# Retention queries and keys turned by SBUF-to-SBUF strip transfers in place of rotation products, with regrouped dense work, earlier input loads and in-place reads

## What is computed

```python
# first block, cut
h = rmsnorm(x); proj = h @ w_in
y_a = chunked_relpos_attention(a_q, a_k, a_v, rel_bias)   # 8 heads of 64
y_b = hgrn2_recurrence(b_q, b_f, b_i, b_g, ...)           # gated recurrence, 8 heads
y_c = mla_attention(c_q, c_kv, c_kr, positions, ...)      # latent attention, 8 heads
x = x + sum(sigmoid(gates) * (y @ w_branch)) @ w_out
x = x + square(relu(rmsnorm(x) @ w_ff1)) @ w_ff2
# second block, two layers, cut
fox  = forgetting_attention(fq, fk, fv, f_logit)
rq_h = apply_rotary(rq); rk_h = apply_rotary(rk) * HEAD_DIM ** -0.5
ret  = silu(rg) * head_group_norm(retention(rq_h, rk_h, rv))
h = h + concat(fox, ret) @ w_out
h = h + gated_conv_ffn(rms_norm(h)) ; h = h + sigmoid(rms_norm(h) @ w_gate) * (p @ w_proj)

def apply_rotary(t, cos, sin):      # halves of 32 of each head of 64
    t1, t2 = split(t)
    return concat([t1 * c - t2 * s, t1 * s + t2 * c])
```

## Time and profile before

| | us |
|---|---|
| median of three runs | 2422.09 |
| lowest, highest | 2421.88, 2429.56 |
| the profiled execution | 2421.89 |
| its span, first to last instruction | 2420.1 |
| granted TensorE clock over the span | 0.995 |
| first matmul | 14.11 |
| first attention | 87 to 217 |
| recurrence | 222 to 359 |
| latent attention | 404 to 527 |
| forgetting attention, layer 1 and 2 | 1061 to 1198, 1767 to 1904 |

### The profile page before, as it was taken

The page is one execution under the profiler, slowest core; times in us unless marked ns, Lnnn a source line. Parts: engine busy times, 40 slices in busy tenths (PEclk is TensorE's granted clock), DMA queues, the critical chain, the costliest instruction groups (busy, mean ns, idle before and its releaser), DMA issues.

```text
span 2420.1 us, 35839 instructions
## 1 busy us (share of the span) xinstructions
PE 2362.6 (98%) x11542; PEld 1861.7 (77%) x11542; DVE 1109.2 (46%) x1851; ACT 883.2 (36%) x1377; POOL 1193.1 (49%) x1572
## 2 busy tenths in 40 slices
PE   7998999999999999999999999999999999999997
PEld 5776776667888888877778888887877678888885
DVE  4366765433323214536664334344346655242444
ACT  3355444444322223424433222245334243222254
POOL 5344554235564455543326555466533245555564
PEclk9999999999999999999999999999999999999998
DMA  4221112114332232321313323323322223323232
GB/s 152 91 86 45 44 53 66 53 53 130 96 113 89 94 104 87 99 96 61 98 43 104 104 88 103 94 81 104 105 70 62 88 70 97 112 87 104 85 93 92
DMA packets 62829, 211.49 MB, mean 87 GB/s; under 512 B 7008, under 2 KB 7392, under 8 KB 62736
## 3 DMA queue, kind: packets, MB, share of 16 engines
q1 hardware_dynamic: 56160, 194.27, 25.6%
q10 hardware_dynamic: 6576, 15.97, 2.0%
HBM read 208.06 MB, written 2.16 MB: 87 GB/s over the span
## 4 chain that ended last, share of the span: by engine, by line
PE 37%; issue 32%; POOL 26%; DVE 2%; POOLq 2%; ACT 1%; DMA 1%; DVEq 0%; ACTq 0%; SPq 0%
POOL w_lo L1840 25%; PE acc L270 11%; PE acc L272 10%; PE acc L271 10%; POOLq L1869 1%; PE sc L416 1%; PE po L364 1%; PE pt L346 1%; PE sc L644 0%; DMA raw<-in_w_in 0%; PE acc L625 0%; POOL qcur L1866 0%; DVE act_lo L1224 0%; PE sc L468 0%; DVEq L1314 0%
## 5 line engine op out<-in xcount | busy, mean ns | idle before, releaser
L1840 POOL TENSOR_TENSOR w_lo<-raw,w_hi 128x256 fp32r<-128x256 f32 x1506 | 1146.1, 793 | 1198.1 <-ACT w_hi L736 1196.2
L270 PE MATMUL acc<-act_hi,w_hi 128*128 128x512 f32 x1768 | 715.0, 404 | 20.3 <-DVE act_lo L1224 15.5
L272 PE MATMUL acc<-act_hi,w_lo 128*128 128x512 f32 x1768 | 691.1, 391 | 0.0
L271 PE MATMUL acc<-act_lo,w_hi 128*128 128x512 f32 x1768 | 690.2, 390 | 0.0
L736 ACT CAST w_hi<-raw 128x1024 fp32r<-128x1024 f32 (+1 forms) x390 | 392.3, 1016 | 380.1 <-PE acc L272 201.0
L270 PE MATMUL acc<-y_hi,w_hi 128*128 128x512 f32 x1108 | 446.3, 403 | 0.9 <-POOL w_lo L1840 0.9
L272 PE MATMUL acc<-y_hi,w_lo 128*128 128x512 f32 x1108 | 432.1, 390 | 0.0
L271 PE MATMUL acc<-y_lo,w_hi 128*128 128x512 f32 x1108 | 431.6, 390 | 0.0
L270 PEld LDWEIGHTS acc<-act_hi,w_hi 128*128 128x128 f32 x1768 | 332.5, 188 | 109.2 <-issue 33.5
L272 PEld LDWEIGHTS acc<-act_hi,w_lo 128*128 128x128 f32 x1768 | 332.6, 188 | 71.1
L271 PEld LDWEIGHTS acc<-act_lo,w_hi 128*128 128x128 f32 x1768 | 333.3, 189 | 65.5 <-issue 2.9
(11 more groups left out here) (313 smaller groups left out, 2113.3 us busy)
## 6 DMA issues: line engine op xcount, KB each, us to landing
raw<-in_w_ffn_wide SPq DMA_DIRECT2D x120, 512.0 KB, 3.5
raw<-in_w_in SPq DMA_DIRECT2D x104, 512.0 KB, 3.5
raw<-in_w_rest SPq DMA_DIRECT2D x72, 512.0 KB, 3.5
raw<-in_w_gate SPq DMA_DIRECT2D x24, 512.0 KB, 3.5
raw<-in_w_ple_gate SPq DMA_DIRECT2D x16, 512.0 KB, 3.5
raw<-in_w_branch SPq DMA_DIRECT2D x24, 256.0 KB, 2.7
raw<-in_w_ffn_narrow SPq DMA_DIRECT2D x16, 384.0 KB, 3.0
x<-in_x ACTq DMA_DIRECT2D x16, 256.0 KB, 3.6
```

Source lines behind the costliest of these rows:

```text
L270: nc.tensor.matmul(dst, w[0], src[0], start=start, stop=False)
L271: nc.tensor.matmul(dst, w[0], src[1], start=False, stop=False)
L272: return nc.tensor.matmul(dst, w[1], src[0], start=False, stop=stop)
L1840: last = nc.gpsimd.tensor_tensor(w_lo[:, slot, cut], raw[:, slot % 2, cut], w_hi[:, slot, cut], ALU.subtract)
```

## The change

- **Rotation.** `rope_r` and its products are gone. After evacuating q (or k) VectorE frees the bank; ScalarE's queue issues four DMAs of 32 partitions by 512 tokens from `wa` to `swapped` with the halves of each head exchanged; VectorE waits for all four, multiplies t by cos and the exchanged rows by sin (the sign of the first half is in the table now) and adds. q is turned at step 3 (was 2), k at step 4 (was 3), ahead of the gate's evacuation. The table `tab` stays the rotary one for the whole attention, so the first decay tile goes to `wb` and is loaded ahead of the attention.
- **Grouping.** A step of `softmax_pair` on TensorE is now: outputs of the tile before the last, scores, transposes of head 0, one share, transposes of head 1, one share.
- **In place.** The recurrence reads values and queries where they lie; no copies. Silu of the last pair moves after level 2 of pair 0.
- **Latent attention.** Sigmoids move to step 1 and totals to step 2 of the next pair.
- **Inputs.** SP issues the first two weight loads, four tiles of x and the constants ahead of its wait. The first `w_lo` is VectorE's, and the second cast comes after two tiles of the norm.

```diff
@@ -125,7 +125,7 @@
              [alias("s_ret2", "act_hi", [P, 1280]), alias("s_ret3", "act_hi", [P, 1280], skip=1280 * 4)]]
-    decay_tile = [tab] + [alias(f"decay{p}", "act_lo", [P, 2, T], skip=(p - 1) * 2 * T * 4) for p in range(1, PAIRS)]
+    decay_tile = [wb[:, 2:4, :]] + [alias(f"decay{p}", "act_lo", [P, 2, T], skip=(p - 1) * 2 * T * 4) for p in range(1, PAIRS)]
     v_ret = [vcur[:, :, :], kcur[:, 0, :].rearrange("p (t f) -> p t f", f=P)]
@@ -136,7 +136,7 @@
     vstage = qcur[:, 1, :]
-    rotated = wb[:, 1, :]
+    swapped = [wb[:, 0, :], wb[:, 1, :]]
     mean_bank = [po[:, :], pt[:, :], sc[:, 0, :], sc[:, 1, :]]
@@ -214,6 +214,14 @@
+    for j in range(2):
+        sp.dma_start(raw[:, j, :], dram["w_in1"][j]).then_inc(raw_loaded[j], 16)
+    for k in range(4, KD):
+        sp.dma_start(x[:, k, :], dram["x"][:, k, :]).then_inc(x_loaded[k], 16)
+    sp.dma_start(consts[:, :, :], dram["consts"]).then_inc(S("const_loaded"), 16)
+    sp.dma_start(masks[:, :, :], dram["masks"]).then_inc(S("const_loaded"), 16)
+    sp.dma_start(positions[:, :], dram["positions"].partition_broadcast(P)).then_inc(S("pos_loaded"), 16)
     sp.wait_ge(started, 1)
@@ -242,7 +250,7 @@
-    load(dram["w_in1"], 0, N_A, N_MA)
+    load(dram["w_in1"][2:N_MA], 0, N_A + 2, N_MA - 2)
     load_groups(4, N_MA, 0)
@@ -366,32 +374,31 @@
         at = 0
-        for qt in range(TT + 1):
-            share = iter(shares[qt])
-            def dense():
-                nonlocal at
-                n = next(share, 0)
-                for i in range(at, at + n):
-                    guest(i)
-                at += n
+        def dense(n):
+            nonlocal at
+            for i in range(at, at + n):
+                guest(i)
+            at += n
+        for qt in range(TT + 2):
+            if qt == 1 and values is not None:
+                pe.wait_ge(S("soft_ofree", 1), pair + 1)
+                transpose_values("soft", pair, po, src)
+            if qt > 1:
+                outputs(qt - 2)
             if qt < TT:
                 scores_of(qt)
-            dense()
-            if qt == 0 and values is not None:
-                pe.wait_ge(S("soft_ofree", 1), pair + 1)
-                transpose_values("soft", pair, po, src)
+            if 0 < qt <= TT:
+                transposes(2 * qt - 2)
+            if qt <= TT:
+                dense(shares[qt][0])
             if rope:
                 rope(qt)
-            if qt:
-                transposes(2 * qt - 2)
-                dense()
+            if 0 < qt <= TT:
                 transposes(2 * qt - 1)
-                dense()
-                outputs(qt - 1)
-                dense()
+                dense(shares[qt][1])
@@ -447,8 +454,8 @@
-    SHARES8 = ((6,), (1, 2, 2, 2), (1, 2, 2, 2), (1, 2, 2, 1), (2, 2, 2))
-    SHARES6 = ((6,), (1, 1, 2, 1), (1, 1, 1, 1), (1, 1, 1, 1), (1, 2, 2))
+    SHARES8 = ((6,), (3, 4), (3, 4), (3, 3), (3, 3))
+    SHARES6 = ((6,), (2, 3), (2, 2), (2, 2), (2, 3))
@@ -472,9 +479,7 @@
         softmax_pair(p, scores_a(p), guest_panels(p * 4 + N_B, N_B), SHARES8, p, src=wv[:, p, :])
-    pe.wait_ge(acc_free, N_MA + 4)
-    pe.wait_ge(S("soft_y"), PAIRS)
-    pe.wait_ge(S("b_qsilu"), PAIRS)
+    pe.wait_ge(acc_free, N_MA + 3)
@@ -485,6 +490,8 @@
                 pe.wait_ge(acc_free, n + 1)
+            if u == 2 and k == 0 and base == 0:
+                pe.wait_ge(S("soft_y"), PAIRS)
             if u == 2 and k == 0 and base == 4:
@@ -503,19 +510,19 @@
     LEVEL_SHARES = (2, 3, 3, 3, 3, 2, 2, 2, 2, 2)
-    with pe.Fori(0, PAIRS) as p:
+    for p in range(PAIRS):
         piece, at = merge_group(p * 4 + N_MA, 0), 0
-        pe.wait_ge(S("b_values"), p + 1)
-        transpose_values("b", p, pt, probs_t[:, 1, :])
+        transpose_values("b", p, pt, wv[:, p, :])
         for v, half in enumerate(LEVELS):
                 pe.wait_ge(S("b_k"), p + 1)
-                pe.wait_ge(S("b_q"), p + 1)
+                pe.wait_ge(S("b_qsilu"), p + 1)
             pe.wait_ge(S("b_sfree", 1), p * n_levels + max(v, 1))
             if v == 1:
+                pe.wait_ge(S("soft_ofree", 1), PAIRS + 1)
                 pe.wait_ge(S("b_ofree", 1), p + 1)
@@ -524,7 +531,7 @@
                     if half == 0:
-                        keys, queries = kcur[rows, 0, t * P:(t + 1) * P], tab[rows, 0, t * P:(t + 1) * P]
+                        keys, queries = kcur[rows, 0, t * P:(t + 1) * P], wa[rows, p, t * P:(t + 1) * P]
                     else:
@@ -618,22 +625,16 @@
-            def rope_r(qt):
-                if qt in (2, 3):
-                    j = qt - 2
-                    pe.wait_ge(S("r_qk"), pair * 2 + (j + 1))
-                    nc.tensor.matmul(acc[:, (O_R + j) % 4, :], c["rope"], wa[:, p + 4 * j, :],
-                                     start=True, stop=True).then_inc(S("r_rot"), 1)
                          SHARES8,
-                         pair + 4, src=wv[:, p, :], rope=rope_r)
+                         pair + 4, src=wv[:, p, :])
         pe.wait_ge(acc_free, layer + (N_BLOCK1 + O_O + 4))
             pair = l * 4 + p
+            pe.wait_ge(S("r_rotused"), pair * 2 + 2)
             if p:
@@ -722,11 +723,8 @@
     act.dma_start(params[:, :], dram["params"]).then_inc(S("param_loaded"), 16)
-    for k in range(KD):
+    for k in range(4):
         act.dma_start(x[:, k, :], dram["x"][:, k, :]).then_inc(x_loaded[k], 16)
-    act.dma_start(consts[:, :, :], dram["consts"]).then_inc(S("const_loaded"), 16)
-    act.dma_start(masks[:, :, :], dram["masks"]).then_inc(S("const_loaded"), 16)
-    act.dma_start(positions[:, :], dram["positions"].partition_broadcast(P)).then_inc(S("pos_loaded"), 16)
     act.wait_ge(started, 1)
@@ -834,10 +832,11 @@
     high(0, 0, 0)
-    high(0, 0, 1)
     act.wait_ge(S("param_loaded"), 16)
         norm_tile(0, k, k % 2, "mix_g")
+        if k == 1:
+            high(0, 0, 1)
     three_more(0, 0, N_A)
@@ -870,10 +874,8 @@
         in_place(ACT.Ln, "b_mixed", "b_mixedlog", p, tmp)
-    if qt == 4:
-        in_place(ACT.Silu, "b_g", "b_gsilu", p, wb[:, p + 4, :])
-        nc.scalar.activation(wa[:, p, :], wa[:, p, :], ACT.Silu).then_inc(S("b_qsilu"), 1)
-        ln_exp_table()
+    if qt == 4 and not last:
+        silus_b(p)
@@ -886,12 +888,6 @@
-    def values_b(p):
-        nc.scalar.copy(probs_t[:, 1, :], wv[:, p, :]).then_inc(S("b_values"), 1)
-    def queries_b(p):
-        nc.scalar.copy(tab[:, 0, :], wa[:, p, :]).then_inc(S("b_q"), 1)
@@ -913,22 +909,18 @@
             nc.scalar.activation(e1, src, ACT.Exp).then_inc(S("b_e"), 1)
+            if n == 2 and not p:
+                silus_b(PAIRS - 1)
             if n == 2 and p:
                 key_b(p + 1)
-            if n == 6 and not last:
-                values_b(p + 1)
-        if not last:
-            act.wait_ge(S("b_s", 1), p * n_levels + 10)
-            queries_b(p + 1)
-    act.wait_ge(S("soft_pv", 1), 4 * PAIRS + 1)
+    act.wait_ge(S("b_keyed"), PAIRS)
+    settle(act)
     key_b(0)
-    values_b(0)
-    queries_b(0)
     for p in range(PAIRS):
@@ -989,17 +981,21 @@
     act.drain().then_inc(S("c_v"), 1)
-    with act.Fori(0, PAIRS) as p:
+    def gates_mb(p):
+        for j in range(2):
+            in_place(ACT.Sigmoid, "m_z", "m_gate", p * 2 + (8 + j), tab[:, j, :])
+        ln_exp_table()
+    for p in range(PAIRS):
         def gates_and_weights(qt):
                 high(p * 2, p * 4, N_MB + LOOK + j, 512 if j < 2 else 1024)
-            if qt == 4:
-                for j in range(2):
-                    in_place(ACT.Sigmoid, "m_z", "m_gate", p * 2 + (8 + j), tab[:, j, :])
-                ln_exp_table()
+            if qt == 1 and p:
+                gates_mb(p - 1)
         softmax_pair(p + 4, gates_and_weights)
+    gates_mb(PAIRS - 1)
@@ -1055,6 +1051,7 @@
     act.dma_start(tab[:, :, :], dram["rotary"]).then_inc(S("rotary_loaded"), 16)
+    act.dma_start(decay_tile[0], dram["decay"][0]).then_inc(S("decay_loaded0"), 16)
     act.wait_ge(S("cum_stored"), l * 32 + 32)
@@ -1070,10 +1067,13 @@
                 aug_rows(p + 1)
-            if qt == 4 and last:
-                act.wait_ge(S("r_rotused"), l * 8 + 8)
-                settle(act)
-                act.dma_start(tab[:, :, :], dram["decay"][0]).then_inc(S("decay_loaded0"), 16)
+            if qt in (2, 3):
+                j = qt - 2
+                act.wait_ge(S("r_qk"), pair * 2 + (j + 1))
+                for to in range(0, P, HD // 2):
+                    at = to ^ (HD // 2)
+                    act.dma_start(swapped[j][to:to + HD // 2, :], wa[at:at + HD // 2, p + 4 * j, :]
+                                  ).then_inc(S(f"r_swap{j}"), 16)
             if qt == 4:
@@ -1309,6 +1309,8 @@
     norm_start()
+    dve.wait_ge(hi_done, 1)
+    v.tensor_tensor(w_lo[:, 0, :], raw[:, 0, :], w_hi[:, 0, :], ALU.subtract).then_inc(S("first_lo"), 1)
     for k in range(KD):
@@ -1384,6 +1386,7 @@
                 v.tensor_copy(key, less)
+                dve.drain().then_inc(S("b_keyed"), 1)
```

(37 more changed lines are left out.)

4 lines of the change are left out of this document (added).

## The result

| | before | after |
|---|---|---|
| median of the runs, us | 2422.09 | 2410.48 |
| lowest, highest | 2421.86, 2429.56 | 2406.44, 2412.73 |
| the profiled execution, its span | 2421.89, 2420.1 | 2412.61, 2410.7 |
| granted clock, mean of the span | 0.995 | 0.991 |

The ratio of after to before is 0.9945, 95% interval 0.9929 to 0.9961. The forecast was 2396.4 us, a gain of 25.5; the gain is 11.6 (9.3 between the two profiled executions), and the time lies 1.5 us above the upper end of the range. The direction was right, the size less than half.

A forecast was written before the change was run, and what follows sets the result against it. TensorE, with matmuls in flight for 98% of the span, was taken to bound the kernel. The terms −4.2 −6.3 +1.0 −2.7 +0.9 −13.8 −7.6 +7.2 summed to −25.5: 2396.4 us, range 2383 to 2409.

The forecast's parts named there:

- start: Input loads and first casts: ScalarE issues fewer loads, first matmul near 9.3 instead of 14.11; 4.2 us gained, between 2 and 6.
- first attention to level 1: Last attention outputs to the recurrence's level 1: values read in place, nothing but PE precedes the transposes; 6.3 us gained, bounds 3 and 7.
- Silu in pair 0: Recurrence pair 0: the last pair's gates, now after level 2, cost 1.0 us, between 0 and 2.
- latent borders: Latent attention's pair borders: waits for the exponential go, −2.7 us; VectorE late at tile 3's row maximum, +0.9.
- rotation products: Forgetting attention: sixteen products of 0.86 us go from TensorE, −13.8 us; called the surest term.
- grouping: All 16 attention pairs: 112 fewer borders of dense work at 0.07 us each, −7.6 us, between 0 and −24.
- border stop: Forgetting attention's pair borders: keys' turn delays VectorE's last evacuation; PE stalls 1.2 us at six borders, +7.2, between 0 and 12.
- (b): Rival: the exchange's four strips land in series, k two us past VectorE's need in all eight pairs; +16, 2412 us; chance 0.11.
- (a): Rival: no border stall in forgetting attention, and dense borders cost more than 0.07 us; 2385 us; chance 0.17.
- (c): Rival: slower than before, VectorE waiting at least 4.1 us for each of eight exchanges of k; up to 2457 us; chance 0.04.
- (d): Rival: start gains nothing (bytes bound it), level 1 waits for VectorE; +2.2 and +3.3, 2402 us; within the forecast's 0.68.
- The likeliest case: The forecast itself, whole kernel, together with (d): 2392 to 2404 us; chance 0.68.

The follow-up runs named there:

- early_old_latent: turn_early with gates and sums of the latent attention back behind the last step of each pair: 2395.22 us, ratio 0.9876.
- parts_products: low_parts with the rotation by products put back and no exchange: 2397.59 us, ratio 0.9882.
- early_old_groups: turn_early with TensorE's order and shares of before in every attention pair, 16 dense pieces instead of 9: 2403.02 us, ratio 0.9906.
- turn_early: The changed kernel with the exchange and the sums that follow it one query block earlier: 2394.73 us, ratio 0.9876.
- parts_gate_first: low_parts with VectorE evacuating the gates ahead of turning the keys at block 4: 2401.44 us, ratio 0.99.
- after_again: The changed kernel unedited, run again beside the others: 2408.57 us, ratio 0.9934.
- low_parts: The changed kernel with GpSimd's last weight panel of each recurrence pair in four quarters behind levels 6 to 9: 2398.07 us, ratio 0.9892.
- early_parts: The changed kernel with both the edits of turn_early and low_parts: 2383.45 us, ratio 0.9822.

## Why the prediction was right in direction and wrong in size

The terms of the sum, in us; "measured" is from the profiles of before and after, or from the run named.

| term | forecast | measured |
|---|---|---|
| start | −4.2 | −3.9 (first attention at 82.82, before 86.68) |
| first attention to level 1 | −6.3 | −6.5 |
| Silu in pair 0 | +1.0 | +2.0 |
| latent borders (−2.7 and +0.9) | −1.8 | −1.7 (early_old_latent) |
| rotation products | −13.8 | −13.6 (parts_products) |
| grouping | −7.6 | −8.3 (early_old_groups) |
| border stop | +7.2 | +11.9 |
| stretches at 1.2 GHz | none | +10.7 |

The second is counted up to level 1 of the recurrence: it comes 13.1 us sooner than before, the last attention pair 5.9, and 0.7 of the difference is grouping. The third is pair 0 from there to its end. The border stop is 6 × 1.98 (below). The stretches are 2.8 + 3.1 + 4 × 1.6 = 12.3, less the 1.6 of the one that the kernel before had behind its first forgetting attention. The measured column gives −9.4, with the 0.8 that the two latent edits bring only together −10.2; the last matmuls of the two traces differ by 9.7.

*What held.* Start, transition, products, grouping and latent borders came out within 1 us each in these profiles. The start is less certain than that: with nothing changed in it, the first attention begins between 82.1 and 84.0 us in the profiles here, and there is one profile of before. Silu in pair 0 took its upper bound: pair 0 got the stop of 0.8 us that was priced, and its stop at level 7 went from 0.4 to 1.35 as in the other pairs. Two readings were loose: the waits listed at the outset come to 48 us and not 40, and the wait of the last attention pair is 2.1, for the 2.4 is two waits. The signs came too: the first matmul at 8.73 (9.3 forecast), matmuls without gaps from 18.45 (near 20) and at 2.4 GHz from 21.27, level 1 after 4.3 us at a clock of 1.00, no row of L625. The first 9 us moved 267 GB/s where they had moved 228, and the strips landed 2.0 us after issue at the median, where the params load took 2.2. The Trainium skill's page "DMA: Bandwidth & Descriptors", section "Issuing engines are not separate DMA queues", lets the start gain issue time alone; the gain of 3.9 agrees, but no run here tells it from bytes moved sooner. The same page of the Trainium skill says in "Rules for kernel authors" that transfers to disjoint partition halves serialize. Here each strip landed 2.0 us after its own issue and the issues were 0.65 apart, so the fourth had landed 3.9 us after the first was issued; one whole transfer time after another, as (b) had it, would be 8.

*The step that failed first* is the price of the order on VectorE, 1.2 us per border. The forecast had the last evacuation 1.8 later, with 0.7 of slack. Measured against the moment at which TensorE was ready (1124.59 less its wait of 1.70), the evacuation stands 3.3 us ahead of it, before 5.7, so it came 2.4 later; less the slack of 0.7 that is the wait of 1.7. The keys' turn in front of it makes 1.9 of the 2.4, as forecast (3.2 us from the evacuation ahead of it, before 1.3). The rest is mostly a term that was left out: the turn in the block ahead now takes 3.0 us from 1113.34 to the next evacuation at 1116.35, where it had taken 2.65. The price of the exchange is in it, for the second product of a turn reads the exchanged rows from SBUF where it had read a bank of `acc`. It took 1.21 to 1.22 us in the eight cases in which it started while GpSimd was subtracting, as at 1114.09, and 0.68 in the eight in which GpSimd was idle; before, all sixteen took 0.68, with GpSimd subtracting beside each. And the wait is not all: pairs with a border stop take 34.5 us where those of turn_early take 32.55, so a stop costs 2.0, six times. The forecast also named the chain by evacuation, Silu and exponential as the one strictly in order; by parts_gate_first the row maxima on the same VectorE are as late, and Silu ahead of them takes nothing off the wait.

*The step that was missing* is what a stop does behind itself, a term put at nothing and measured at 10.7 us. I read 0.81 in the gap before the recurrence and priced it away there, but took every other stop at its length alone. The changed kernel has six new ones, five of 1.7 us and one of 1.2, and keeps two of the recurrence's per pair, listed at 0.8 and 1.35 (1.67 in pair 2, 0.74 in the last); behind some of them the clock fell to 1.2 GHz for 3.4 or 6.8 us, in 27.2 us of the profiled execution. The four profiles with border stops (after, after_again, low_parts, parts_gate_first) all have a stretch inside the forgetting attention, the nine others have none there. With the longer of the recurrence's stops gone, in six profiles, none has a stretch in the recurrence. In early_parts, which keeps the shorter one of 0.8, none is left anywhere between start and tail. The length of a stop does not settle it: in eight profiles, that of before among them, a stretch of 3.4 came within 7 us behind a forgetting attention, where the longest listed stop is 0.8. Why the recurrence's stops, which the kernel before had too, drew stretches of 6.8 us in four profiles (the changed kernel twice, turn_early, early_old_latent) and none in three (before, products, early_old_groups) is open; that is too few to call it the change's doing.

*The rivals and the signs.* The forecast's own sign of being wrong came: the forgetting attention is longer than before, by 0.2 us in layer 1 and 1.9 in layer 2. (a), no border stop: false as placed. (b), late strips, gives 2412, close to what was measured, and is false all the same: no wait on a strip. (c) fell with it. (d): the start gained its 3.9. The likeliest case was right in kind, with one term 4.7 short and one of 10.7 missing. On which side of the range's upper end a run falls is up to the stretches: the changed kernel's runs go from 2406.4, inside it, to 2412.7.

## What to carry over

On an engine that is full, price a new stop by its length and by the time behind it: here 1.7 us cost 2.0, and 1.6 to 3 more where the clock fell after it. Removing ten short stops gave 27 us beyond the change and a time that repeats within 0.6 us; here the spread of the runs was itself a sign of stops. Ask of each edit at which block its work stands: the exchange was worth nothing in one place and 14 us one block earlier. And when work moves to another engine's time, look at what runs beside it there.

## What the hardware showed that was not expected

The stretches come in two lengths, 3.4 and 6.8 us, and not at the same places in every execution of one kernel; in the stages where the long stops were removed none was left; TensorE was busy through each of the changed kernel's six. At 1.2 GHz a stretch of 3.4 us cost 1.6 and one of 6.8 cost 2.8 to 3.1. Transfers from SBUF to SBUF of 32 partitions by 2 KB landed 2.0 us after issue at the median, four in a row with no wait on any; what they cost is ScalarE's time to issue, 2.56 us for four and 5.14 for eight of half the size. The same 128x512 product of two SBUF tiles on VectorE (L1703) took 1.21 us beside GpSimd's subtraction and 0.68 with GpSimd idle, eight times each; with one operand in `acc` (L1693 before) it took 0.68 beside GpSimd too, sixteen times. No run moved GpSimd's work to try it.
